# A fifth expert slot, one buffer of gathered tokens, and a re-ordered shared expert in a two-layer MoE trunk

## The reference

```
shared = (silu(x @ sw1) * (x @ sw3)) @ sw2          # every token
s      = sigmoid(x @ router_w); 8 of 64 experts are chosen per token
y[t]  += gate[t,e] * (silu(x[t] @ w1[e]) * (x[t] @ w3[e])) @ w2[e]
x      = LN(alpha * x + shared + y)
```

## Time and profile before

| | us |
|---|---|
| median of 3 runs (lowest, highest) | 1344.71 (1343.71, 1345.81) |
| profiled execution, own time | 1348.52 |
| its span, first to last instruction | 1346.7 |
| PE busy | 1303.1 (97%) |
| DVE, ACT, POOL busy | 475.4, 310.7, 81.0 |
| DMA, mean | 343 GB/s, 462 MB |

### The profile page before, as it was taken

One profiled execution on the slowest core, in us unless ns is written; L12 is line 12 of the kernel. 1 busy time (PEld: TensorE's weight loads), 2 busy tenths in 40 slices (PEclk: granted clock), 3 DMA queues, 4 the chain that ended last, 5 costly groups with the idle time before them and its releaser, 6 DMA issues.

```text
span 1346.7 us, 23086 instructions
## 1 busy us (share of the span) xinstructions
PE 1303.1 (97%) x9730; PEld 750.1 (56%) x9730; DVE 475.4 (35%) x791; ACT 310.7 (23%) x747; POOL 81.0 (6%) x93
## 2 busy tenths in 40 slices
PE   9999999999999899998999999999999999999998
PEld 4555665555555455554498457555555545555544
DVE  1584532333332323323511246232332323333344
ACT  1244322121221221111210234222222221112112
POOL 2443100000000000000100021000000000000000
PEclk9999999999999999999999999999999999999999
DMA  9820679999999999999764527799999999999992
GB/s 305 305 97 32 250 299 419 420 420 421 421 421 420 421 420 422 420 420 385 244 229 147 196 96 278 309 419 421 419 420 421 420 421 421 421 421 421 420 382 78
DMA packets 83151, 462.00 MB, mean 343 GB/s; under 512 B 7024, under 2 KB 7504, under 8 KB 34672
## 3 DMA queue, kind: packets, MB, share of 16 engines
q1 hardware_dynamic: 81040, 454.15, 83.4%
q0 software_dynamic: 2016, 6.43, 1.6%
HBM read 459.50 MB, written 1.05 MB: 342 GB/s over the span
## 4 chain that ended last, share of the span: by engine, by line
PE 77%; DMA 19%; DVE 2%; issue 1%; ACT 0%; POOL 0%; SPq 0%; DVEq 0%; POOLq 0%
PE ps L1259 26%; DMA ring<-in_exp_w_dram 19%; PE ps L1299 12%; PE ps L918 4%; PE ps L1452 4%; PE ps L1321 4%; PE ps L1198 4%; PE ps L1095 3%; PE ps L1022 3%; PE ps L1167 2%; PE ps L1119 2%; PE ps L1269 1%; PE ps L1159 1%; PE ps L1080 1%; PE ps L1431 1%; PE ps L938 1%
## 5 line engine op out<-in xcount | busy, mean ns | idle before, releaser
L1299 PE MATMUL ps<-ring,qkT 128*32 128x512 f32 x1984 | 232.9, 595 | 4.1 <-issue 3.1
L2176 DVE TENSOR_TENSOR o_tok<-ps,o_tok 128x1024 f32<-128x1024 f32 x124 | 150.6, 1223 | 157.4 <-PE ps L1321 157.4
L2181 DVE TENSOR_TENSOR y_lo<-ps,y_hi 128x1024 fp32r<-128x1024 f32 x62 | 75.9, 1224 | 213.7 <-ACT y_hi L1684 213.7
L1259 PE MATMUL ps<-ring,xT 128*64 128x256 f32 x1008 | 124.5, 385 | 15.8 <-DMA ring<-in_exp_w_dram 15.8
L1299 PEld LDWEIGHTS ps<-ring,qkT 128*32 128x32 f32 x1984 | 61.5, 109 | 128.8 <-issue 128.3
L1259 PE MATMUL ps<-ring,pT 128*64 128x256 f32 x992 | 124.3, 385 | 6.7 <-DMA ring<-in_exp_w_dram 6.5
L1659 ACT ACTIVATE roped<-ps 128x256 f32<-128x256 f32 x64 | 24.6, 385 | 456.5 <-PE ps L1259 456.5
L1259 PE MATMUL ps<-ring,proj 128*64 128x256 f32 x1008 | 121.8, 379 | 0.0
L1259 PE MATMUL ps<-ring,gb_row 128*64 128x256 f32 x992 | 121.6, 379 | 0.0
L2165 DVE SCALAR_TENSOR_TENSOR roped<-roped,rows,ps 128x256 f32<-128x256 f32 x64 | 30.8, 481 | 237.4 <-ACT roped L1659 237.4
L1259 PEld LDWEIGHTS ps<-ring,xT 128*64 128x64 f32 x1008 | 71.0, 136 | 74.5 <-issue 34.6
(11 more groups left out here) (308 smaller groups left out, 1469.5 us busy)
## 6 DMA issues: line engine op xcount, KB each, us to landing
ring<-in_exp_w_dram SPq DMA_DIRECT2D x158, 2048.0 KB, 23.3
ring<-in_exp_w_dram SPq DMA_DIRECT2D x54, 1024.0 KB, 9.0
ring<-in_od_w_in_dram SPq DMA_DIRECT2D x6, 2048.0 KB, 8.6
ring<-in_ple_w_gate_dram SPq DMA_DIRECT2D x4, 2048.0 KB, 15.3
ring<-in_ev_w_in_dram SPq DMA_DIRECT2D x3, 2048.0 KB, 19.5
ring<-in_ev_w_o_dram SPq DMA_DIRECT2D x2, 2048.0 KB, 10.0
x_tok<-in_exp_w_dram SPq DMA_DIRECT2D x4, 1024.0 KB, 8.5
ring<-in_exp_w_dram SPq DMA_DIRECT2D x8, 512.0 KB, 15.9
```

The costliest lines, as they stand in the source:

```text
L1259: ins = pe.matmul(ps[b * SLOTS:(b + 1) * SLOTS, 2, w * FE:(w + 1) * FE], xe(odd, c)[:, u * P + b * SLOTS:u * P + (b + 1) * SLOTS], views[b ...
L1299: ins = pe.matmul(ps[q:q + TILE_SLOTS, 4 + half, :], hT[:, f, h0:h0 + TILE_SLOTS], down_rows(b, f, half), start=(f == 0), stop=(f == 1))
L2176: dve.tensor_tensor(ys, ps[:, bank:bank + 2, :], ys, ALU.add).then_inc(sem("y_added"), 1)
L2181: dve.tensor_tensor(y_lo[:, :], ps[:, 4:6, :].rearrange("p b n -> p (b n)"), y_hi[:, :], ALU.subtract)\
```

## The change

Where loads go is now a table. An expert e has a home: one of the ring's four slots, the fifth place (FIFTH), or a sixth one that is used once a layer, for expert 1 (APART: w1 in `o_tok`, that is in `y_acc`; w3 in `qkT`; w2 in `gb_row`). Every fifth expert goes to FIFTH, for which one buffer of gathered tokens was given up (`proj` and `gb_row`); the other is now `xT` with `pT`. All four parts of a gather are done in the last pair of an octet, and ACT may copy them out only when that pair's w3 products are done. All loads are of one expert (1 MB). The w3 products go to bank 3 and `silu` waits for the w1 products alone. The start of `y_acc` moves from ACT to POOL, behind the w1 products of pair 0. The shared expert's up products hold tokens and stream the weights; the activations come out untransposed and are turned in pair 24, and the down products move to pairs 25, 26, 28 and 29. At the program's start the two multiplications with zeros go and the first products start on the first half of the transposed tokens. Several semaphores are merged under new names, which changes no order.

```diff
-UNROLL = 4; EARLY = 2 * RING; AGAIN = EARLY + 2; NEXT_EARLY = AGAIN + RING
+FIFTH = RING
+APART = RING + 1
+EARLY_HOMES = (3, APART, 1, 2, FIFTH)
+CYCLE = (0, 3, 1, 2, FIFTH)
+SHARED_TURN = PAIRS - 8
+SHARED_AT = (PAIRS - 7, PAIRS - 6, PAIRS - 4, PAIRS - 3)
+def home(e):    return EARLY_HOMES[e] if e < len(EARLY_HOMES) else CYCLE[e % len(CYCLE)]
+def room_of(e): return {6: 0, 7: 2, 8: 3}.get(e, e - len(CYCLE))
...
# SP
+            def pair_load(L, m):
+                after = [e for e in range(6, NE) if room_of(e) // 2 == m]
+                whole = [e for e in after if e < NE - 2]
+                sp.wait_ge(sem("exp_gate"), L * PAIRS + m + 1)
+                for e in after: gate_load(L, e)
+                sp.wait_ge(sem("exp_up"), L * PAIRS + m + 1)
+                for e in whole: lin_load(L, e)
+                if NE - 1 in after: last_lin_load(L)
+                sp.wait_ge(sem("exp_down"), L * PAIRS + m + 1)
+                for e in whole: down_load(L, e)
+                if NE - 1 in after: last_down_load(L)
+            def fifth_load(L):
+                sp.wait_ge(sem("router_mm"), NT * (L + 1))
+                sp.wait_ge(sem("x_split"), NT * (L + 1))
+                gate_load(L, 4)
+                sp.wait_ge(sem("shared_w1_used"), L + 1)
+                lin_load(L, 1)
+                sp.wait_ge(sem("gb_used"), NT * (3 * L + 1))
+                down_load(L, 1)
+                sp.wait_ge(sem("shared_h"), NT * (L + 1))
+                down_load(L, 4, (1,))
...
                     if k == e0 + 2:
+                        apart_gate_load(L)        # w1 of expert 1, after the last queries' transposes
                         shared_load(L)
+                        lin_load(L, 4)
+                        down_load(L, 4, (0,))
...                                                # FIFTH's w2: 512 KB, then twice 256 KB
# POOL
+                pool.wait_ge(sem("exp_gate"), L * PAIRS + 1)
+                for t in range(NT):
+                    step(pool.tensor_tensor(y_acc[:, t, :]..., x_hi[:, t, :]..., x_lo[:, t, :]..., ALU.add))
+                    pool.tensor_scalar(y_acc[:, t, :], y_acc[:, t, :], ALPHA, None, ALU.mult).then_inc(sem("y_begun"), 1)
# PE, project_first
                         transpose_tile(x_tok, 0)
-                        multiply_zeros(2)
-                        wait_tile("xT", 3 * L, 0)
+                        wait_chunk(3 * L, 0, 0)
                         chunks(0, 0, 2)
-                        chunks(0, 2, 4)
+                        chunks(0, 2, 3)
                         transpose_tile(x_tok, 1)
+                        chunks(0, 3, 4)
# PE, shared expert
-                            ins = pe.matmul(ps[:, 4 + t, n * P:(n + 1) * P], (shared_w1, shared_w3)[n // 2][:, c, n % 2::2],
-                                            xT[:, c, t * P:(t + 1) * P], start=(c == 0), stop=(c == DC - 1))
+                        ins = pe.matmul(ps[:, 4 + t, w * FE:(w + 1) * FE], xT[:, c, t * P:(t + 1) * P],
+                                        (shared_w1, shared_w3)[w][:, c, :], start=(c == 0), stop=(c == DC - 1))
+                def shared_turn():                # four transposes in pair 24, copied back by DVE
...
# PE, one pair
+                    exp_up(m, o, u, 0)
+                    if scatter_last:         scatter(m - 1, 0, 1 - par)
+                    if m == SHARED_TURN:     shared_turn()
+                    if m in SHARED_AT:       shared_down(SHARED_AT.index(m))
+                    if gathers:              gather(o + 1, 0)          # gathers: u == 3, not in the last octet
+                    exp_up(m, o, u, 1)
+                    if scatter_last:         scatter(m - 1, 1, 1 - par, bank=6 if gathers else 0)
+                    h_transpose(m)
+                    if selT_next:            sel_transpose(m + 1, ...)
+                    if gathers:              gather(o + 1, 1)
+                    exp_down(m, 0, ...)
+                    if gathers:              gather(o + 1, 2)
+                    exp_down(m, 1, ...)
+                    if gathers:              gather(o + 1, 3)
...
# ACT, before the loop and in it
-                x_high(0); copy_T("xT_act", tp, 0); router_exp(0); y_begin(0)
+                copy_T("xT_act", tp, 0); x_high(0); router_exp(0)       # the same for tile 1
+                    silu(m)                                             # waits for exp_gate
+                    if gathers: xe_copy(o + 1, 0)
                     hT_copy(m)
+                    if gathers: xe_copy(o + 1, 1)
                     selT_copy(m + 1, 1 - u % 2)
+                    if gathers: xe_copy(o + 1, 2)
                     y_high(m)
+                    if gathers: xe_copy(o + 1, 3)
# DVE: a semaphore "chosen" in choose(); gate_h also waits for exp_up; sel_build(o + 1) in the octet's first pair
```

More of the change, by code:

```diff
@@ L306, in release_value @@
             return sem(f"ple_mm{L}"), NT * 2 + n if n else NT
[L310 to L325, removed]
+        assert all(expert_item[L] % RING == EARLY_HOMES[0] for L in range(DEPTH))
+        loaded, gate_at, lin_at, down_at = {}, {}, {}, {}
+        gate_total, lin_total, down_total = [0] * (APART + 1), [0] * (APART + 1), [0] * (APART + 1)
+        for k, (parts, (_, L, e)) in enumerate(items):
+            if parts != "expert":
+                lin_total[k % RING] += 16 * len(parts)
+                loaded[k] = lin_total[k % RING]
+                continue
+            at = home(e)
+            gate_total[at] += 16
+            lin_total[at] += 16
+            down_total[at] += 48 if at == FIFTH else 32 if e >= NE - 2 else 16
+            gate_at[L, e], lin_at[L, e], down_at[L, e] = gate_total[at], lin_total[at], down_total[at]
+        w_loaded = [sem(f"w_loaded{s}") for s in range(APART + 1)]
+        down_loaded = [sem(f"down_loaded{s}") for s in range(APART + 1)]
+        w1_loaded = [sem(f"w1_loaded{s}") for s in range(APART + 1)]
         def slot_view(k, n, c):
@@ new lines, in ffn_load, with last_lin_load @@
+            def ffn_load(L, e):
+                gate_load(L, e)
+                lin_load(L, e)
+                down_load(L, e)
+            def last_lin_load(L):
+                s, e = home(NE - 2), NE - 2
+                for half in range(2):
+                    cols = slice(half * UP_N // 2, (half + 1) * UP_N // 2)
+                    sp.dma_start(ring[:, s:s + 2, UP_N + cols.start:UP_N + cols.stop],
+                                 a["exp_w3"][L, e:e + 2].rearrange("e (p c) f -> p e (c f)", c=DC)[:, :, cols])\
+                      .then_inc(w_loaded[s + half], 16)
@@ new lines, in last_down_load @@
+            def last_down_load(L):
+                s, e = home(NE - 2), NE - 2
+                for half in range(2):
+                    cols = slice(half * PIECE, (half + 1) * PIECE)
+                    for b in range(2):
+                        w2 = ring[:, s + b, DOWN0:DOWN0 + 2 * D].rearrange("p (c f) -> p c f", c=2)
+                        sp.dma_start(w2[:, :, cols], a["exp_w2"][L, e + b].rearrange("(p c) f -> p c f", c=2)[:, :, cols])\
+                          .then_inc(down_loaded[s + half], 16)
@@ L565, in _ @@
+                    if k == e0 + RING:
+                        fifth_load(L)
+                        for m in range(PAIRS - 2):
+                            pair_load(L, m)
                         k = e0 + NE
@@ L2227, in dve_step @@
                         y_low(m)
-                    if build_bf and u == 2:
+                    if gather_next and u == 2:
                         sel_bf_build(o + 1)
```

557 lines of the change are left out of this document (244 added, 313 removed).

## The result

The changed kernel takes **1368.08 us**, median of 4 runs (1366.44 to 1369.86); the kernel before, beside it, 1345.26 (1343.71 to 1346.4). The ratio is 1.0167, with a 95% interval from 1.0153 to 1.0181: 22.8 us slower, where 5.9 us faster was forecast. A second set of runs of the same kernel gave 1366.7 us, ratio 1.0147 (1.0123 to 1.0171).

What follows compares the result with a forecast made beforehand. The weight stream was taken to set each loop's end, TensorE 2 us behind as a bound. Gains of 0.9 at the start and 2.5 in each loop sum to 5.9 us: span 1340.8, 1338.8 on the runs' scale, range 1334.8 to 1344.6.

Steps and rivals of the forecast that it cites:

- Part 3: TensorE's own time in the loop: octets of 56.2 us against 55.2, pair 31 reachable at 619.3 to 620.4 us.
- 13.79 - 1.08 + 0.35 = 13.06 us: Pair without gather: the earlier pair's time, less a gather part, plus idle TensorE in front of exp_down.
- The last octet of before has just this order: Reason for 0.35 us idle TensorE ahead of exp_down: the earlier kernel's last octet already shows it.
- A pair with gathers ... 17.03: Pair doing all four gather parts: 12.71 + 4 x 1.08 = 17.03 us, the parts covering both waits.
- Rival c: TensorE's new order binds, through waits ahead of exp_down or ACT's queue; 0.3 us a pair gives 1354.2 us; chance 0.12.
- Parts 1 and 2: Weight stream in the loops: 3.8 us lead from a sixth early expert, less 1.3 for smaller loads, 2.5 a layer.
- part 2: Stream rate with 1 MB loads: 0 to 2.6 us lost a layer, 1.3 taken; last pair's w1 at 621.9 us.
- the bytes left behind that w1 are the same 4.2 MB, and the last pair's steps are the same: End of the loop: after the last pair's w1 lands, the remaining steps take the same 12.85 us.
- the whole lead of 2.5: Each loop was to end 2.5 us earlier, the stream's lead of 3.8 less 1.3.
- Part 4: Ahead of the loops: start 0.1 us later, bounds 0.6 earlier and 1 later; y_begin on POOL 11.5 us, hidden.
- Part 5: Program's start: the first projection ends at 22.2 us in place of 23.1, 0.9 us earlier, bounds 0 and 1.1.

Runs made afterwards that it cites:

- run 2: The changed kernel with the two waits for w2 ahead of exp_down made one, both experts of a pair on one semaphore; 1361.65 us.
- run 3: The changed kernel with one more wait ahead of exp_down, for a semaphore long reached; 1366.03 us.
- run 5: The changed kernel with both scatters behind the w3 products in pairs without gathers; 1360.59 us.
- run 9: run 6 with ACT's x_high back ahead of the copies of xT, y_begin staying on POOL; 1351.72 us.
- run 6: run 5 with the shared expert's turn and four down products moved early, to pairs 4, 5, 6, 8 and 9; 1359.44 us.
- run 10: run 9 with loads called by whole pairs from pair 20 on; 1341.85 us.
- run 4: The changed kernel with ACT's x_high back ahead of the copies of xT; 1360.61 us.
- run 1: The changed kernel again, unaltered; 1366.7 us.
- run 7: run 6 with x_high ahead of the copies of xT and y_begin taken from POOL (sums on DVE, scalings on ACT); 1356.91 us.
- run 8: The kernel before with only the new order of the first projection and the place products released by `chosen`; 1344.72 us.
- run 11: run 10 with the two waits for w2 ahead of exp_down made one; 1337.09 us.

## Why the prediction was wrong, step by step

The span was forecast at 1340.8 us and measured at 1367.2. Of these 26.4 us, 23.9 lie between the end of the attention and the end of the loop, over both layers, 3.7 in the tail and 0.3 at the start; 1.5 go off again, since the profile before had a stretch at the lower clock.

**Part 3, TensorE's own time, is the step that failed**, and it turned the sign. "13.79 - 1.08 + 0.35 = 13.06 us" is 13.33 measured. The 0.27 are: 0.15 for a fourth wait ahead of exp_down (runs 2 and 3), which the sentence "The last octet of before has just this order" overlooked, since there one signal served two experts and only three waits stand; 0.08 that I read from the earlier trace rows too low, since the 0.35 us are counted from the end of the sel products and not from the next step's usual start (the octet's rows give 1.02 from h transposes to exp_down, I had summed 0.95); and 0.04 of waiting for the gate product. The last octet differs in one thing more: both scatters stand behind the w3 products there. Its pair 28 lasts 12.78 us from start to start; a fourth wait makes that 12.93, the pair of run 5, and the scatters parted, as the changed kernel has them, 13.33. "A pair with gathers ... 17.03" is 17.48: four times 0.07 for a gather that stands alone between other shapes, 0.14 for exp_down in two halves, and the 0.04. An octet is 57.5 us, not 56.2. Besides, the ple transposes wait 1.1 us for the last copy of xe, which now ends right ahead of them, and each shared part makes the gate product 0.1 later. Sum for layer 0: 7 x 1.3 + 1.1 + 0.4 and 1.3 for the later start make 11.9; pair 31 starts at 632.0, where the text had 619.3 to 620.4.

Rival c came nearest: "TensorE's new order binds". It had 0.12. Its room of 0.13 us a pair was passed, and its 0.3 us a pair is what the octet's 1.3 us come to, 0.33. Its place holds only about half of them: 3 x 0.23 us ahead of exp_down; the rest is the gather parts, exp_down in halves and the gate product, and ACT's queue of four copies never bound. Its time, 1354.2, is still 14 us too low. " have measured just this wait" was the reason for so small a chance, and it compared the order of instructions but not their waits.

**Parts 1 and 2, the stream, were right in their numbers**, hidden in the changed kernel and seen once TensorE was out of the way. In run 9 w1 of the last pair landed at 620.1 us with a loop start of 177.0; the forecast, 621.9 for a start of 178.5, says 620.4. The rate was 419 GB/s against 421, 0.5% less, where 1.3 us in 430, 0.3%, was taken.

**One step of part 2 was right in its words and wrong in what it left out**: "the bytes left behind that w1 are the same 4.2 MB, and the last pair's steps are the same". What counts ahead of that w1 is when pair 30 can run. With five places and pairs of two, w1 of a pair's second expert stands behind w3 and w2 of its first, which are needed only later in the pair: 2.1 MB, 5.0 us. In runs 6 and 9 the last pair starts 4.4 to 4.7 us behind the landing of its w1, and taking the cause away gave back 4.2 and 3.6 us (run 10), more than the whole lead of 2.5. So with TensorE's time as forecast, the kernel would still not have been 5.9 us faster. An estimate from run 9, whose pairs of 12.93 us are faster than the forecast's 13.06: its loops are 1.6 and 1.9 us longer than those of the kernel before, and with 0.9 gained at the start that makes about 3 us slower.

**Part 4, ahead of the loops**: "I take 0.1 later; the bounds are 0.6 earlier and 1 later". It is 2.1 later in each layer, outside the bounds. Counted from the end of the first projection, in layer 0: the second tile's exp came 1.4 us later, not 0.3 to 0.5 (0.8 by the clock of the trace, and the start was 0.6 earlier); POOL's x_lo, moved along with x_high, fell on DVE's chain, 1.2 us; the place products, started on `chosen`, gave 0.7 back, contrary to the text; and 0.15 were lost behind the one-hot matrices. Most of the 1.4 is the same fault once more: the first tile's choice is held up too (its first DVE operation takes 1.31 us, to the end of POOL's first x_lo), so DVE begins the second tile's norm late, where it had waited 0.98 us for TensorE before and now doesn't. I had counted the ACT instruction that was moved and not the POOL instruction that it releases. The Trainium skill, "SBUF — State Buffer", section "Who interferes with whom", says that an operation of VectorE in its two-port mode and one of GpSimd exclude each other for a whole instruction; the trace agrees (1.42 us, ending with x_lo; 0.20 without), though no row names the mode, and I had not weighed it.

y_begin on POOL started at 184.63, since `o_tok` is expert 1's w1 until then, and took 13.3 us, not 11.5. In layer 0 it was hidden; in layer 1 of the profiled execution the gate product of pair 1 came 0.64 us late behind it, in the traces of the other runs at most 0.04.

**Part 5, the start**: 0.6 us in the profile after, 0.9 forecast. Over the twelve traces that have the new start the first projection ends between 21.5 and 23.1 us, at 22.0 in the middle, against 22.95 in the one trace of the kernel before; so the forecast holds, as far as one trace before can tell.

**Behind loop 1**, nothing was forecast and 3.7 us were lost. Between the last scatter and the ple products TensorE stands still for 2.0 us, and then works for 3.4 us at the lower level of its clock (a granted clock of 0.5; products start 0.85 us apart in place of 0.43), which costs 1.7; the ple products in the timeline, and the window around them, whose granted clock is the third number from the end:

```profile
1325.11 8.80 PE L1426 MATMUL ps<-ring,p_tok 128*128 128x512 f32 x16 [2.02 <-issue]
```
```profile
1321.00:1330.00 9.00, 6.94 (x20) 2.74 (x17) 7.40 (x14) 2.08 (x3) 0.00 (x0) 0.81 0.68 237
```

The idle time is 0.5 to 0.8 us in runs 3, 4, 5 and 10, 1.4 in run 1, 1.9 to 2.1 in runs 7 and 9 and 5.8 in run 6; it is nothing in the kernel before and in runs 2, 8 and 11, and in layer 0 always. In all nine traces that have it a 16 KB transfer of the instruction queue ends 1.5 to 1.6 us before TensorE goes on. That TensorE waits there for its own program, behind a branch, fits, and so does it that runs 2 and 11, with some 60 waits less in that program, are free of it; but it was not tested, and why it is longer in one execution than in another stays open.

## What to carry to other kernels

When an order of instructions is judged by a stretch that already has it, compare the waits in front of each instruction and the shapes on both sides too, and sum from start to start, not from idle times. When a ring's size is no multiple of what is consumed at once, write down the order in which bytes arrive next to the order in which they are needed; one place more can deliver later. And follow a moved instruction to whom it releases: here an ACT copy took a POOL operation with it into DVE's critical chain.

## What the runs showed of the hardware

- Four semaphore waits ahead of exp_down cost TensorE 0.15 us more than three (1.18 us against 1.03), a fifth nothing, when all but one have long been reached; the profile shows it as "issue" or puts it on the engine waited for.
- Groups of TensorE products with other tile sizes cost more when they alternate: w1 and w3 products on end take 7.06 us, parted by a scatter 2 x 3.60; two scatters on end 1.12, apart 2 x 0.67; a gather part 1.08 with the h transposes, of the same 128 x 128 size, behind it, else 1.14 to 1.15. That the change of size is the cause was not tested by itself.
- x_lo on POOL held a DVE operation of 0.20 us for 1.42 us (1.31 in the first tile), until its own end.
- Loads of 1 MB, landing 17 to 28 us after their issue, ran at 418 to 419 GB/s in the changed kernel (415 to 419 in run 10 from 225 us on, with the last pieces 412), loads of 2 MB at 421.
- TensorE's granted clock fell to 0.5 for 3.4 us at a time (6.8 in run 6) in some executions. In the tail it did so behind idle time of 2.0 us (the changed kernel), 2.1 (run 7) and 5.8 (run 6), and not behind 1.4 (run 1) or 1.9 (run 9).
